# Where the second output projection is computed: inside the last head or behind it

## The reference, cut to what matters

```python
h_lat, h_ctx = mlstm_bidir(p_lat, p_ctx, ...)                 # 4 heads of width 128, both directions
mix = concatenate([mlstm_out(h_lat, gate, head_norm),          # rows 0..3 of 8 blocks of 128: one per head
                   pool_mixer(p[..., M_COLS:], pool_w, ...)])  # rows 4..7
x = ada_out(x, mix @ w_out, mod, 1, norm_post[l, 1], 1.0)      # the second output projection
```

## Time and profile before

| | us |
|---|---|
| median of 3 runs | 3063.39 (3062.98 to 3068.55) |
| the profiled execution | 3060.69 |
| its span | 3058.8 |
| PE busy in the span | 2976.5 |
| mean granted clock of PE | 0.992 of full speed |

### The profile page before, as it was taken

One profiled execution on the slowest core, in us unless ns is written; L12 is line 12 of the kernel. 1 busy time (PEld: TensorE's weight loads), 2 busy tenths in 40 slices (PEclk: granted clock), 3 DMA queues, 4 the chain that ended last, 5 costly groups with the idle time before them and its releaser, 6 DMA issues. The chain is left out here.

```text
span 3058.8 us, 36237 instructions
## 1 busy us (share of the span) xinstructions
PE 2976.5 (97%) x14776; PEld 2502.4 (82%) x14776; DVE 1790.9 (59%) x2590; ACT 1127.5 (37%) x1686; POOL 221.2 (7%) x184
## 2 busy tenths in 40 slices
PE   8999999999999999999999999999999988899998
PEld 6888878888878888888888899888898865788886
DVE  7766656765867767667757555323366655443234
ACT  4433332434434333324424344222244565332221
POOL 0300000000001101100000020000020024100000
PEclk9999999999999999999999999999999999999999
DMA  8454455443433333344444344222244320123321
GB/s 293 148 171 142 135 176 179 143 140 131 144 117 131 131 128 122 101 150 134 143 143 145 111 147 146 98 97 97 98 148 130 106 97 1 55 90 97 97 97 62
DMA packets 107781, 383.83 MB, mean 125 GB/s; under 512 B 11964, under 2 KB 13372, under 8 KB 107616
## 3 DMA queue, kind: packets, MB, share of 16 engines
q1 hardware_dynamic: 83856, 296.51, 29.1%
q10 hardware_dynamic: 23760, 85.01, 8.5%
HBM read 379.37 MB, written 2.10 MB: 125 GB/s over the span
## 5 line engine op out<-in xcount | busy, mean ns | idle before, releaser
L1784 DVE TENSOR_TENSOR WL<-stage,WH 128x1024 fp32r<-128x1024 f32 x508 | 631.2, 1245 | 585.1 <-ACT WH L1186 584.6
L451 PE MATMUL ps<-HH,WH 128*128 128x512 f32 x2184 | 855.6, 392 | 8.0 <-DVE HL L1830 4.7
L452 PE MATMUL ps<-HL,WH 128*128 128x512 f32 x2184 | 852.2, 390 | 0.0
L453 PE MATMUL ps<-HH,WL 128*128 128x512 f32 x2184 | 852.0, 390 | 0.0
L1186 ACT ACTIVATE WH<-stage 128x1024 fp32r<-128x1024 f32 x512 | 536.7, 1052 | 418.8 <-PE ps L453 409.3
L451 PE MATMUL ps<-GH,WH 128*128 128x512 f32 (+2 forms) x1649 | 572.4, 347 | 6.4 <-DVE WL L1784 3.3
L452 PE MATMUL ps<-GL,WH 128*128 128x512 f32 (+2 forms) x1649 | 569.0, 345 | 0.0
L453 PE MATMUL ps<-GH,WL 128*128 128x512 f32 (+2 forms) x1649 | 568.9, 345 | 0.0
L451 PEld LDWEIGHTS ps<-HH,WH 128*128 128x128 f32 x2184 | 411.6, 188 | 92.1 <-DVE HL L1830 4.9
L453 PEld LDWEIGHTS ps<-HH,WL 128*128 128x128 f32 x2184 | 411.1, 188 | 86.1
L452 PEld LDWEIGHTS ps<-HL,WH 128*128 128x128 f32 x2184 | 411.7, 188 | 83.0
(11 more groups left out here) (249 smaller groups left out, 2853.7 us busy)
## 6 DMA issues: line engine op xcount, KB each, us to landing
stage<-ws SPq DMA_DIRECT2D x535, 512.0 KB, 3.4
MST<-wm ACTq DMA_DIRECT2D x154, 512.0 KB, 3.4
Z<-wm SPq DMA_DIRECT2D x10, 512.0 KB, 8.0
TAB<-consts ACTq DMA_DIRECT2D x7, 448.0 KB, 3.5
MST<-wm SPq DMA_DIRECT2D x6, 512.0 KB, 7.4
out<-X SPq DMA_DIRECT2D x8, 256.0 KB, 2.1
X<-xT SPq DMA_DIRECT2D x4, 256.0 KB, 4.6
X<-xT ACTq DMA_DIRECT2D x4, 256.0 KB, 5.1
```

Of the source, the lines that this page charges most:

```text
L451: e.matmul(o, wh, mh, start=start, stop=False, **more)
L452: e.matmul(o, wh, ml, start=False, stop=False, **more)
L453: return e.matmul(o, wl, mh, start=False, stop=stop, **more)
L1784: e.tensor_tensor(wl, src, wh.bitcast(F32), ALU.subtract).then_inc(wlo.sem, wlo.up(("w", i)))
```

## The change

The function `early_tile(nn)` is replaced by `early(*units)`, which takes single units (nn, k). Twelve units, k = 0, 1, 4, 5, 6 and 7 of tiles 0 and 1, are issued inside head 3: two at each of c = 2, 3 and 4 between `scores` and `sums(3, c-1)`, two before `sums(3, 4)`, two before `sums(3, 5)`, two before `denominators(3)`. Behind the head, PE runs k = 2 of tiles 0 and 1; `normalize(3, 0)`; k = 0, 1, 2 of tile 2; `normalize(3, 1)`; k = 4 to 7 of tile 2; `head_sums(3)`; seven units of tile 3; `rms_last`; seven units of tile 4; k = 3 of tiles 0 to 4; and tiles 5 to 7 whole. The number of units stays 64. ACT and DVE now split chunks D and E behind the denominators (`weights(("early", 1, 7), ahead=2)`) and chunk F behind `normalize(3, 0)` and before `normalize(3, 1)` (`weights(("early", 2, 7))` in the loop over d; in its second turn there is nothing left for it); no split stands before `head_norm`.

```diff
--- before.py
+++ after.py
@@ -1086,6 +1086,28 @@
             pool_out(2)
             scores(0, 0)
             pool_out(3)
+            def early(*units):
+
+                for nn, k in units:
+                    p = PS[WOB[nn]]
+                    if k == 0:
+                        if nn < 2:
+                            pe.wait_ge(dv, "nrm", NH - 2, nn)
+                        elif nn < 4:
+                            pe.wait_ge(dv, *SCORE_OF[max(SCORE_OF) - (1 if (max(SCORE_OF) % 2) != nn % 2 else 0)], 1)
+                        else:
+                            pe.wait_ge(dv, "nrm", NH - 1, nn - 4)
+                    pe.wait_ge(lo, *(("po", k - 4) if k > 3 else ("mix", k)))
+                    wh, wl = block(("w_out2", 0, k * 128, nn * 128))
+                    inst = mm3(p[:, :], wh, wl, *hx(k), k == 0, k == 3)
+                    if k == 3:
+                        ended(inst, ("wo", nn))
+                    elif cur["used"] == 8:
+                        ended(inst)
+                    upto[("early", nn, k)] = cur["n"]
+
+
+            beside = [(nn, k) for nn in range(2) for k in (0, 1, 4, 5, 6, 7)]
             for h in range(NH):
                 more = h + 1 < NH
                 for c in range(5):
@@ -1094,6 +1116,8 @@
                         normalize(h - 1, c)
                     elif 2 <= c < 4 and more:
                         running_max(h + 1, c - 2)
+                    if c >= 2 and not more:
+                        early(*beside[2 * c - 4:2 * c - 2])
                     if c:
                         sums(h, c - 1)
                     if c == 3 and h:
@@ -1104,41 +1128,32 @@
                     stat_free()
                     q_and_k(h + 1, 0, STAT)
                     stat["free"] = (lo, ("qk", h + 1, 0))
+                else:
+                    early(*beside[6:8])
                 sums(h, 4)
                 if more:
                     q_and_k(h + 1, 1, score_bank("qk", h + 1, 1))
                     q_and_k(h + 1, 2, score_bank("qk", h + 1, 2))
+                else:
+                    early(*beside[8:10])
                 sums(h, 5)
                 if more:
                     scores(h + 1, 0)
+                else:
+                    early(*beside[10:12])
                 denominators(h)
 
-            def early_tile(nn):
-                p = PS[WOB[nn]]
-                if nn < 2:
-                    pe.wait_ge(dv, "nrm", NH - 2, nn)
-                else:
-                    pe.wait_ge(dv, *SCORE_OF[max(SCORE_OF) - (1 if (max(SCORE_OF) % 2) != nn % 2 else 0)], 1)
-                for k in (0, 1, 2, 4, 5, 6, 7):
-                    pe.wait_ge(lo, *(("po", k - 4) if k > 3 else ("mix", k)))
-                    wh, wl = block(("w_out2", 0, k * 128, nn * 128))
-                    inst = mm3(p[:, :], wh, wl, *hx(k), k == 0, False)
-                    if cur["used"] == 8:
-                        ended(inst)
-                upto[("early", nn)] = cur["n"]
-
-            early_tile(0)
-            for d in range(2):
-                normalize(NH - 1, d)
-                early_tile(1 + d)
+            early((0, 2), (1, 2))
+            normalize(NH - 1, 0)
+            early((2, 0), (2, 1), (2, 2))
+            normalize(NH - 1, 1)
+            early((2, 4), (2, 5), (2, 6), (2, 7))
             head_sums(NH - 1)
-            early_tile(3)
+            early(*[(3, k) for k in (0, 1, 2, 4, 5, 6, 7)])
             rms_last(("hn", NH - 1), S, dv, "hn1", NH - 1)
-            for nn in range(4):
-                pe.wait_ge(lo, "mix", 3)
-                wh, wl = block(("w_out2", 0, 3 * 128, nn * 128))
-                ended(mm3(PS[WOB[nn]][:, :], wh, wl, *hx(3), False, True), ("wo", nn))
-            for nn in range(4, 8):
+            early(*[(4, k) for k in (0, 1, 2, 4, 5, 6, 7)])
+            early(*[(nn, 3) for nn in range(5)])
+            for nn in range(5, 8):
                 if nn < 6:
                     pe.wait_ge(dv, "nrm", NH - 1, nn - 4)
                 else:
@@ -1730,17 +1745,16 @@
                     exponents(h + 1, 0)
                 denominators(h)
 
-            weights(("early", 0))
+            weights(("early", 1, 7), ahead=2)
             for d in range(2):
                 normalize(NH - 1, d)
-                weights(("early", 1 + d))
-            weights(("early", 3))
+            weights(("early", 2, 7))
             head_norm(NH - 1)
             for i in range(4):
                 sa.hand(i, lo, "mix", NH - 1)
             for nn in range(8):
                 weights(("wo", nn))
-                if nn >= 4:
+                if nn > 4:
                     walk.tick()
                 act.wait_ge(mm, "wo", nn)
                 act.wait_ge(dv, "hn2", NH - 1)
```

## The result

The changed kernel takes 3048.59 us (median of 4 runs, 3047.19 to 3050.14) where the kernel before takes 3063.89 (4 runs, 3062.98 to 3068.55). The ratio is 0.9947, 95% interval 0.9935 to 0.996: 12 to 20 us faster by that interval, 15.3 by the medians. The forecast was 3053.6 with a range of 3050.5 to 3057.5: the sign was right, the gain was undersized and lay outside the range.

The account below looks back on a forecast made before the run. PE was taken as the bound, busy 2976.5 of 3058.8 us, so only its idle or low-clock time could be won. Tail terms of -11.24 us and +1.4 for its later start gave -9.8: 3063.39 to 3053.6, range 3050.5 to 3057.5.

Parts of the forecast that it names:

- The new wait for the split of F: Before `head_sums(3)` in the tail: PE stalls while ACT and DVE split F before copying the second spreads; +2.5 us.
- the lower clock behind it: Tail, behind the stall before `head_sums(3)`: one stretch of 3.4 us at half clock; +1.7 us.
- The base: Kernel before: profiled execution of 3060.69 us taken as the base, with the runs' median a constant 2.7 us above it.
- Twelve units into the head: Head 3: moved units shorten the tail by 8.16 us, while the tail starts 1.4 us later.
- The clock at the start of the tail: First 12 matmuls of the projection: full clock instead of the lower one, 2.36 us saved.
- Tile 4 ahead of the wait: Tail, at `mix, 3`: seven units cover the stall, -3.20 us, and the lower clock behind it goes, -1.72.
- The splits of D and E: ACT and DVE behind the denominators: hidden, with 0.3 us of slack on DVE; uncovered 1 us at most.
- The first: Rival for the tail: no lower clock behind the new stall before `head_sums(3)`; -11.5 us, 3051.9; chance 0.18.
- The second: Rival: longer low clock behind the new stall (+1.6) or a fall in the head (+1.7); 3055.3 to 3056.9; chance 0.20.
- The third: Rival for head 3: the twelve units cost 8.16 us there, not 1.4; 3060.4, no difference; chance 0.09.
- The fourth: Rival: clock stays low from the new stall to the end of tile 7; +13.8 us, 3077; chance 0.03.

Follow-up runs that it names:

- e1: Changed kernel with the split of chunk F put between the two normalize steps on ACT and DVE; 3054.24 us, ratio 0.9964 to the kernel before.
- b2: The kernel before, unchanged, executed once more for its trace; 3064.12 us.
- b4: The kernel before, unchanged, another single execution for its trace; 3065.88 us.
- e7: Kernel before plus 19 matmuls whose result nobody reads, in four holes of head 3; 3059.34 us, ratio 0.9984.
- e2: Kernel before with only tile 4, without its k = 3, moved ahead of the wait for `mix, 3`; 3058.8 us, ratio 0.9981.
- e3: Changed kernel with tile 4 put back behind the wait for `mix, 3`, the twelve units staying in head 3; 3053.41 us, ratio 0.9963 to the kernel before.
- e5: Changed kernel with the pair of units before `sums(3, 3)` put behind `rms_last`, so four stand before `sums(3, 4)`; 3048.61 us.
- e6: Changed kernel with four units before `sums(3, 3)`, so ahead of `rms_last`, and none before `sums(3, 4)`; 3051.21 us.
- b3: The kernel before, unchanged, another single execution for its trace; 3068.95 us.

## Why the prediction was wrong

*The new wait for the split of F (+2.5) and the lower clock behind it (+1.7)* is the step that failed. It came from a misread indentation. The changed kernel has no such wait; e1, which has it, shows 2.34 us of it and the lower clock, 3.87 us in all. Without both, and with 0.2 for what `head_sums` still waits, the prediction's sum is -13.8; the profiled stretch shows -13.36. By the prediction's own way to the median that is 3063.39 - 13.8 = 3049.6, 1.0 above the measured median and still below the lower end of the range, 3050.5.

*The base* is the second step, a term that the sum did not have. The prediction took the clock of head 3 before as the one profiled execution shows it. Its stretch was 82.30 us; three others took 83.91 to 87.08. A sum made on it is too small by the mean of what the others lose there, 85.0 - 82.3 = 2.7 us. The gap of 2.7 us between the profiled execution and the median of the runs stood in the prediction and was carried over as a constant. It was not one: by b2 to b4, more of the difference lies in what the change removes than elsewhere. That the two numbers are alike is chance: the four profiled executions lie 4.2 us above the first on average, 2.7 of it in the stretch and 1.5 outside. With both corrections: -13.8 - 2.7 = -16.5, so 3063.89 - 16.5 = 3047.4, measured 3048.59, now 1.2 too low; the correction is an estimate from four executions.

*Twelve units into the head*: right. The head became 1.75 us longer (29.10 against 27.35), where the transposes were forecast 1.56 later. Each pair fell as forecast: counted from the transposes of head 2, the sums come 0.84 us later at c = 2, 0.03 at c = 3 and 1.42 at c = 4, where 0.8, 0 and 1.36 were forecast, and the hole left before the last sums is 1.05 of the 1.1 named.

*The clock at the start of the tail* (-2.36): right, and shown apart from the moved work by e7 (2.40 on the tail). *Tile 4 ahead of the wait* (-3.20 and -1.72): right, 5.15 on the tail in e2. The tail as a whole went from 54.95 to 39.84, by -15.11; the terms without the wait make -8.16 - 2.36 - 3.20 - 1.72 + 0.2 = -15.24. *The splits of D and E*: hidden, with 0.42 us between DVE's second low part and the product that waits for ACT.

*The rivals.* The first, no lower clock behind the stall, came nearest in its number (3051.9), but not in its reason, as there was no stall. The second, with the rule of the Trainium skill ("TensorE: Matmul & The Clock Gate", section "A second HAM failure mode: psum-queue depth-cycling") on idle times between groups of matmuls, did not come for the changed head, which is at full clock in both executions, as it is in e1, e3, e5 and e6. The traces of the kernel before agree with the rule: the clock of its head fell once in one of the four executions and twice in the others. The prediction used it for a fall in the new kernel alone, where it spoke against the change; used for further falls in the old one it would have widened the range to the right side. The third (the head pays for every unit, 8.16 us) is ruled out: the head pays 1.75 for twelve units, and 0.43 in e5. The fourth did not occur.

## What to carry to other kernels

Where PE has many small holes in a row, look at the clock in more than one execution before a sum is made on it: here the holes cost their length plus stretches at the lower clock whose number and length differed from execution to execution. Filling them with matmuls of no use removed the second cost (e7), filling them with work that has to be done removed both. Fill them behind the matmul on which the other engines' chain waits and not ahead of it: one pair of units made the head 1.33 us longer ahead of `rms_last` than behind it, of the 1.36 that it takes. And when a forecast turns on where in an engine's order a wait stands, read the nesting of the line that puts it there.

## What the runs showed of the hardware

Four executions of one program, with the same instructions and the same releasers, gave the head a mean granted clock of 0.97, 0.91, 0.82 and 0.83, and lengths of 27.35, 29.22, 31.99 and 31.29 us. Before the first fall in b3 there was no long stop: PE had holes of 0.38, 0.45 and 1.33 us and was busy in between. The hole before the sums of c = 5 is 2.01 us in the first execution and 2.36, 2.52 and 2.56 in b2, b3 and b4. In b3 this goes with a longer chain, 5.94 us from the spreads of `rms_last`, which ran at the lower clock, to these sums. In b2 and b4 that time is 5.08, as in the first execution (5.09), so there PE was only through earlier with the work that stands between. With the holes filled the clock stayed full in the head, in six profiled executions with projection units (of which e6 still had holes of 1.17 and 1.05 us) and in one with matmuls whose result nobody reads (e7); and the two executions of the changed kernel agreed in the whole stretch to 0.01 us.
